# Two weight loads of the first mixer's compression issued on SyncE's queue instead of ScalarE's

## The chip, the cores and the metric

The kernel runs on one core of a Trainium2 chip. The metric is the device time of one execution in microseconds, the median of the runs of one program. TensorE (PE in the profile), VectorE (DVE), ScalarE (ACT), GpSimd (POOL) and SyncE (SP) each run their own instruction list and meet only at semaphores. Loads from device memory are issued by SP, ACT or POOL and moved by the core's 16 DMA engines.

## The reference, cut to what matters

The program is a stack of transformer-like blocks over 256 tokens of width 1024 in float32. The change lies in the first mixer, `nsa_attention`. It projects the normed input with one large weight matrix, and two of the results are compressed by a small network whose first weights are `w1_k` and `w1_v`, 2048 x 256 each, 2 MB apiece in float32:

```
proj = h @ w_in                      # 1024 x 2608, loaded in 11 pieces ("units")
q, kc, vc, ks, vs, kwn, vwn, gl = jnp.split(proj, splits, axis=-1)
def compress(t, pe, w1, w2):
    blk = t[:, tok_idx] + pe[:, None, :]
    blk = jnp.moveaxis(blk, 3, 2).reshape(B, n_c, N_KV, CMP_BLOCK * HEAD_DIM)
    return jax.nn.gelu(blk @ w1) @ w2
k_cmp = compress(kvh(kc), pe_k, w1_k, w2_k)
v_cmp = compress(kvh(vc), pe_v, w1_v, w2_v)
```

After this mixer come a feed-forward block, a second mixer with its feed-forward block, and a second model part of the same kind. None of that is touched.

## The kernel before

All large weights stream through one ring of three buffers of 1 MB (`RAW`, in the profile `raw_units`). A piece of weights is a unit, numbered over the whole program. Units 0 to 10 are those of `a_in`, the first mixer's projection: eight of 1 MB, then unit 8 of 192 KB (the gates), then two more of 1 MB. Each unit passes four stations in order:

- SP issues its load in `load_unit`; from unit 3 on it first waits for `lo_done`, the split of the unit three places earlier, because that frees the buffer.
- ACT copies it to a rounded high part in `split_hi` (line 170, `units_hi`), when it has landed and when TensorE has finished the unit three before.
- DVE subtracts to get the low part in `split_lo` (line 178, `units_lo`).
- TensorE multiplies: 48 matmuls per unit at lines 195 to 197, three per product.

ACT and DVE take their work strictly in the order written out in `project_a_scalar` and `project_a_vector`. There, the splits of units 3 and 4 come ahead of the copies of the first results out of PSUM (line 1083 on ACT, line 1136 on DVE), and TensorE waits for both copies before unit 4, since that unit's result overwrites the bank: `pe.wait_ge(m.s("a_left_out"), 1)` and `pe.wait_ge(m.s("a_right_out"), 1)` in `project_a_tensor`.

The compression's weights `W1K` and `W1V` are not part of the ring; they have their own place in SBUF. They are waited for once, in `compress_hidden_tensor` (line 216), which TensorE reaches after unit 7: `pe.wait_ge(m.s("w1_in"), 32)`. In the kernel before, ACT issues both loads in `compress_loads_scalar`, after it has copied the distance tables (lines 893 and 895) and ahead of the split of unit 3.

At the very start SP issues the two halves of x and units 0 to 2 with no wait. ACT at the same time issues nine small loads (the identity, the table inputs, seven rows of gains at line 829), and only then loads its function table and squares x for the norm (line 241). POOL issues some twenty small loads of constants.

Of the kernel before, what the change touches and what calls it, by code (L numbers as in the profile page):

```python
# [17 lines left out]
P = 128  # L18
# [67 lines left out]
def slot(n):  # L86
    return n % 3
# [57 lines left out]
def first_unit(stage):  # L145
    return [n for n, u in enumerate(UNITS) if u[0] == stage][0]
# [7 lines left out]
def load_unit(sp, m, n, parts):  # L154

    if n >= 3:
        sp.wait_ge(m.lo_done, n - 2)
    assert len(parts) == UNITS[n][1], (n, UNITS[n])
    for dst, src in parts:
        sp.dma_start(dst, src).then_inc(m.raw_landed[slot(n)], 16)  # L160
# [69 lines left out]
def norm_squares_scalar(act, m, k, src, junk, ready, tiles=range(TT)):  # L230

    sem, value, per_tile = ready
    n = TT * ROW_NORMS[k][0]
    for t in tiles:
        act.wait_ge(sem, value + per_tile * t)
        if junk is None:
            out = m.HN[:, t, :]
        else:
            out = junk
            act.wait_ge(m.s("norm_squared"), n + t)  # L240
        act.activation(out, src[:, t, :], ACT.Square,
                       accum_out=m.SS[:, t:t + 1]).then_inc(m.s("norm_squared"), 1)
# [42 lines left out]
def norm_turned_scalar(act, m, k, g, outs, second=0, gains=False):  # L285

    if gains:
        act.wait_ge(m.s("gains_set"), 1)
    for b in range(4):
        act.wait_ge(m.s("norm_transposed"), 4 * ROW_NORMS[k][0] + b + 1)  # L290
        if second:
            act.wait_ge(m.s("norm_lo"), ROW_NORMS[k][1] + b + 1)
        for kt in (2 * b, 2 * b + 1):
            hi, src = turned_rows(m, k, g, b, kt, outs[0][:, kt, :])
            ins = act.activation(hi, src, ACT.Copy, scale=m.GC[:, g * KT + kt:g * KT + kt + 1])
        ins.then_inc(m.s("norm_hi"), 1)
# [521 lines left out]
def first_loads_scalar(act, m):  # L818

    i = m.i  # L820
    act.dma_start(m.IDENT[:, :], i["c_ident"]).then_inc(m.s("ident_in"), 16)
    act.dma_start(m.HOT, i["c_hot"]).then_inc(m.s("table_inputs_in"), 16)
    gains = [(i["norm_mix"], 2), (i["norm_ffn"], 2), (i["kv_norm"], 1), (i["ffn1_norm_2"], 1), (i["mem_norm_2"], 1),
             (i["mix_norm_2"], 1), (i["ffn2_norm_2"], 1)]
    assert len(gains) == N_GAINS
    g = 0
    for src, n in gains:
        rows = src.rearrange("(k p) -> k p", p=P) if len(src.shape) == 1 else src.rearrange("g (k p) -> (g k) p", p=P)
        act.dma_start(m.GROW[g * KT:(g + n) * KT, :], rows).then_inc(m.s("gains_in"), 16)
        g += n  # L830
# [8 lines left out]
    pool.dma_start(m.RBI[:, :], i["rel_bias_2"]).then_inc(m.s("table_rows_in"), 16)  # L839


def compress_loads_scalar(act, m):

    i = m.i
    for dst, src in ((m.A.W1K, i["a_w1_k"]), (m.A.W1V, i["a_w1_v"])):
        act.dma_start(dst, src[0].rearrange("(u p) n -> p u n", p=P)).then_inc(m.s("w1_in"), 16)


def setup_vector(dve, m):
# [38 lines left out]
def tables_scalar(act, m):  # L888

    act.wait_ge(m.s("tables_made"), 2)  # L890
    w = W_ALL // 3
    for c in range(3):
        act.activation(m.TAB16[:, c * w:(c + 1) * w], m.pb[4 + c][0:HEADS, 0:w], ACT.Copy)\
            .then_inc(m.s("tables_copied"), 1)
    act.activation(m.TAB8, m.pb[7][0:8, 0:W_IDX], ACT.Copy).then_inc(m.s("tables_copied"), 1)
# [59 lines left out]
def project_a_sync(sp, m):  # L955
    w = m.i["a_w_in"][0].rearrange("(k p) n -> p k n", p=P)
    n = first_unit("a_in")
    for c in range(5):
        if c == 4:
            load_unit(sp, m, n, [(m.RAW[:, slot(n), 0:KT * 48].rearrange("p (k c) -> p k c", k=KT),  # L960
                                  w[:, :, 2560:2608])])
            n += 1
        for half in range(2):
            load_unit(sp, m, n, [(m.RAW[:, slot(n), :].rearrange("p (k c) -> p k c", k=4),
                                  w[:, 4 * half:4 * half + 4, c * 512:(c + 1) * 512])])
            n += 1


def project_keys_a_tensor(pe, m, n, bank):
# [531 lines left out]
def attend_a_scalar(act, m):  # L1501
    def out_hi(T):
        act.wait_ge(m.s("a_summed"), 2 * (LAST_PAIR[T] + 1))
        act.activation(m.OTH[:, T, :], m.pb[6 + T % 2][:, 0:S], ACT.Copy).then_inc(m.s("a_out_hi"), 1)

    for p in range(2, NPA + SUM_AFTER):
        for T in range(7):
            if LAST_PAIR[T] + 4 == p:
                out_hi(T)
        if p < NPA:  # L1510
            exp_pair_a_scalar(act, m, p)
        if TURN_AFTER <= p < NPA + TURN_AFTER:
            i = p - TURN_AFTER
            for par in range(2):
                act.wait_ge(m.s("a_turned"), 2 * i + par + 1)
                if i >= 2:
                    act.wait_ge(m.s("a_summed"), 2 * (i - 1))
                act.activation(m.A.PT[:, i % 2, par, :], m.pb[4 + par][:, 0:3 * P], ACT.Copy)\
                    .then_inc(m.s("a_turned_copied"), 1)
    out_hi(7)  # L1520
# [1915 lines left out]
def hybrid_transformer_kernel(nc, i, out):  # L3436
    with ExitStack() as ctx:
        m = Names()
# [25 lines left out]
        @block.sync  # L3464
        def _(sp):
            first_loads_sync(sp, m)
            project_a_sync(sp, m)
            out_sync(sp, m, "a_out", i["a_w_out"][0])
            ffn_sync(sp, m, 0, i["ffn_w_up"][0], i["ffn_w_down"][0])
            project_b_sync(sp, m)  # L3470
            out_sync(sp, m, "b_out", i["b_w_out"][0])
            ffn_sync(sp, m, 1, i["ffn_w_up"][1], i["ffn_w_down"][1])
            ffn_sync(sp, m, 2, i["ffn1_w_in_2"][0], i["ffn1_w_out_2"][0])
            memory_sync(sp, m)
            project_c_sync(sp, m)
            merge_sync(sp, m)
            mixer_out_sync(sp, m)
            ffn_sync(sp, m, 3, i["ffn2_w_in_2"][0], i["ffn2_w_out_2"][0])
            for t in range(TT):
                store_half(sp, m, out, t, 0)  # L3480
            sp.wait_ge(m.s("stored"), 16 * 2 * TT)
# [35 lines left out]
        @block.scalar  # L3517
        def _(act):
            first_loads_scalar(act, m)
            for t in range(TT):  # L3520
                norm_squares_scalar(act, m, 0, m.XR, None, (m.x_in[t], 16, 0), (t,))
            split_ahead(act, m, split_hi, "a_in", 0, 1)
            norm_turned_scalar(act, m, 0, 0, HT, gains=True)
            split_ahead(act, m, split_hi, "a_in", 1, 3)
            tables_scalar(act, m)
            compress_loads_scalar(act, m)
            project_a_scalar(act, m)
            attend_a_scalar(act, m)
            split_ahead(act, m, split_hi, "a_out", 1, 4)
            split_ahead(act, m, split_hi, "ffn0", 0, 2)  # L3530
            tile_scalar(act, m, 0)
            ffn_scalar(act, m, 0)
            split_ahead(act, m, split_hi, "b_in", 0, 2)
            norm_halves_scalar(act, m, 2, 2)
            norm_turned_scalar(act, m, 2, 4, HT)
            project_b_scalar(act, m)
            attend_b_scalar(act, m)
            split_ahead(act, m, split_hi, "b_out", 1, 4)
            split_ahead(act, m, split_hi, "ffn1", 0, 2)
            tile_scalar(act, m, 1)  # L3540
            ffn_scalar(act, m, 1)
            split_ahead(act, m, split_hi, "ffn2", 0, 2)
            state_step_scalar(act, m)
            tile_scalar(act, m, 2)
            ffn_scalar(act, m, 2)
            norm_turned_scalar(act, m, 5, 6, HT)
            split_ahead(act, m, split_hi, "mem_kv", 0, 2)
            norm_halves_scalar(act, m, 6, 6)
            split_ahead(act, m, split_hi, "c_in", 0, 1)
            norm_turned_scalar(act, m, 6, 7, OT)  # L3550
            memory_scalar(act, m)
            split_ahead(act, m, split_hi, "c_in", 1, 2)
            state_turn_scalar(act, m)
            inner_c_scalar(act, m)
            mix_c_scalar(act, m)
            split_ahead(act, m, split_hi, "c_out", 2, 4)
            split_ahead(act, m, split_hi, "ffn3", 0, 2)
            tile_scalar(act, m, 3)
            ffn_scalar(act, m, 3)
            final_norm_scalar(act, m)  # L3560
            for t in range(TT):
                store_half(act, m, out, t, 1)
# [75 lines left out]
def split_ahead(eng, m, split, stage, first, last):  # L3638

    for j in range(first, last):  # L3640
        split(eng, m, first_unit(stage) + j)
# [29 lines left out]
```

## Time and profile before

| | us |
|---|---|
| median of 3 runs | 1306.37 |
| lowest, highest run | 1306.25, 1306.43 |
| span of the profiled execution | 1303.1 |
| median less the span | 3.3 |
| TensorE busy in the span | 1270.1 |
| VectorE, ScalarE busy | 811.3, 644.9 |
| ScalarE's issue of the second load of compression weights | 4.92 |

Only the span is known of the profiled execution; its own device time is not listed, so the 3.3 us outside the span are taken from the median of the runs. Three runs lie within 0.2 us of each other. All times below count from the span's start. The first mixer takes the first 144 us.

### The profile page before, as it was taken

Reading aid. Unit: us, or ns where it says so; the run is one execution under the profiler, and the core shown is the slowest. Engines: PE = TensorE matmul, PEld = TensorE weight load, DVE = VectorE, ACT = ScalarE, POOL = GpSimd, SP = SyncE. Lnnn points to the kernel's source line nnn. Section 1 sums busy time; section 2 is a strip of 40 time slices with the busy share of each in tenths; the row PEclk is TensorE's granted clock in tenths of the full one; section 3 lists DMA queues with packets and bytes.
Section 4 is the critical chain, followed back from the end, with each engine's and each line's share of the span. In section 5 each row is a group of like instructions: output and inputs, shape, how many; then the busy total and the mean of one; then the engine's idle time right before and its main releaser. Section 6 shows DMA issues by size and latency. Waiting matters only on the chain.

```text
span 1303.1 us, 19302 instructions
## 1 busy us (share of the span) xinstructions
PE 1270.1 (97%) x7279; PEld 1059.4 (81%) x7279; DVE 811.3 (62%) x1210; ACT 644.9 (49%) x946; POOL 271.3 (21%) x362
## 2 busy tenths in 40 slices
PE   6999999999999999999999999999999999999997
PEld 5986788888799977888888788888887778888886
DVE  3468675555574486654555755556789877755554
ACT  4438654444453366543444655445444683544442
POOL 6420210000000041102000489701186210200000
PEclk9999999999999999999999999999999999999999
DMA  9970556555455644467655465654544436556651
GB/s 288 273 136 19 166 173 193 182 184 186 159 194 180 177 115 130 161 195 175 228 183 179 167 194 186 220 188 147 194 130 146 146 121 202 181 190 193 191 188 41
DMA packets 155883, 224.77 MB, mean 172 GB/s; under 512 B 13395, under 2 KB 107979, under 8 KB 155820
## 3 DMA queue, kind: packets, MB, share of 16 engines
q1 hardware_dynamic: 141008, 208.36, 50.9%
q0 software_dynamic: 10064, 10.54, 4.3%
q10 hardware_dynamic: 4748, 5.02, 1.1%
q8 instruction: 41, 0.67, 0.2%
q14 instruction: 22, 0.18, 0.0%
HBM read 222.56 MB, written 1.25 MB: 172 GB/s over the span
## 4 chain that ended last, share of the span: by engine, by line
PE 80%; DVE 8%; ACT 4%; DMA 4%; issue 2%; POOL 1%; SPq 0%; DVEq 0%; ACTq 0%; POOLq 0%
PE bank L195 23%; PE bank L197 23%; PE bank L196 23%; PE bank L216 4%; DMA raw_units<-in_a_w_in 3%; DVE units_lo L178 3%; PE bank L204 2%; PE bank L702 1%; DMA raw_units<-in_ffn_w_up 1%; ACT arena L1497 1%; DVE arena L2907 1%; PE bank L211 1%; PE bank L1774 1%; DVE arena L2898 1%; ACT units_hi L170 1%
## 5 line engine op out<-in xcount | busy, mean ns | idle before, releaser
L621 DVE TENSOR_TENSOR units_lo<-raw_units,units_hi 128x2048 fp32r<-128x2048 f32 x96 | 223.1, 2324 | 154.2 <-ACT units_hi L575 154.2
L195 PE MATMUL bank<-units_hi,turned_hi 128*128 128x512 f32 (+1 forms) x792 | 307.0, 388 | 3.1 <-DVE units_lo L178 1.3
L197 PE MATMUL bank<-units_hi,turned_lo 128*128 128x512 f32 (+1 forms) x792 | 302.1, 381 | 0.0
L196 PE MATMUL bank<-units_lo,turned_hi 128*128 128x512 f32 (+1 forms) x792 | 301.7, 381 | 0.0
L178 DVE TENSOR_TENSOR units_lo<-raw_units,units_hi 128x2048 fp32r<-128x2048 f32 (+2 forms) x103 | 232.4, 2265 | 109.3 <-ACT units_hi L170 109.1
L170 ACT ACTIVATE units_hi<-raw_units 128x2048 fp32r<-128x2048 f32 (+2 forms) x103 | 193.2, 1886 | 113.3 <-PE bank L197 83.1
L575 ACT ACTIVATE units_hi<-raw_units 128x2048 fp32r<-128x2048 f32 x96 | 183.5, 1911 | 104.0 <-PE bank L197 95.6
L195 PE MATMUL bank<-units_hi,second_hi 128*128 128x512 f32 (+1 forms) x560 | 219.2, 391 | 0.0
L197 PE MATMUL bank<-units_hi,second_lo 128*128 128x512 f32 (+1 forms) x560 | 216.8, 387 | 0.0
L196 PE MATMUL bank<-units_lo,second_hi 128*128 128x512 f32 (+1 forms) x560 | 216.6, 387 | 0.0
L195 PEld LDWEIGHTS bank<-units_hi,turned_hi 128*128 128x128 f32 x792 | 149.0, 188 | 32.8 <-DVE units_lo L178 3.0
L197 PEld LDWEIGHTS bank<-units_hi,turned_lo 128*128 128x128 f32 x792 | 148.9, 188 | 29.2
L196 PEld LDWEIGHTS bank<-units_lo,turned_hi 128*128 128x128 f32 x792 | 149.2, 188 | 26.9
L195 PEld LDWEIGHTS bank<-units_hi,second_hi 128*128 128x128 f32 x560 | 105.4, 188 | 23.4 <-issue 1.7
L197 PEld LDWEIGHTS bank<-units_hi,second_lo 128*128 128x128 f32 x560 | 105.3, 188 | 21.6
L196 PEld LDWEIGHTS bank<-units_lo,second_hi 128*128 128x128 f32 x560 | 105.6, 189 | 20.5
L585 ACT ACTIVATE second_hi<-bank 128x512 fp32r<-128x512 f32 x44 | 26.3, 599 | 127.6 <-PE bank L702 127.6
L261 POOL TENSOR_SCALAR means<-sums 128x1 f32<-128x1 f32 x6 | 2.1, 357 | 363.4 <-ACT rows L249 363.4
L627 DVE SCALAR_TENSOR_TENSOR rows<-rows,bank 128x256 f32<-128x256 f32 x88 | 36.9, 419 | 57.3 <-ACT rows L581 42.0
L635 DVE TENSOR_TENSOR second_lo<-bank,second_hi 128x512 fp32r<-128x512 f32 x44 | 30.4, 690 | 66.6 <-ACT second_hi L585 66.6
L195 PE MATMUL bank<-second_hi,units_hi 128*128 128x256 f32 x240 | 68.3, 285 | 0.0
L196 PE MATMUL bank<-second_lo,units_hi 128*128 128x256 f32 x240 | 67.9, 283 | 0.0
(352 smaller groups left out, 1789.8 us busy)
## 6 DMA issues: line engine op xcount, KB each, us to landing
raw_units<-in_ffn_w_up SPq DMA_DIRECT2D x88, 512.0 KB, 4.8
raw_units<-in_ffn_w_in SPq DMA_DIRECT2D x88, 512.0 KB, 4.6
raw_units<-in_ffn_w_down SPq DMA_DIRECT2D x22, 1024.0 KB, 4.9
raw_units<-in_ffn_w_out SPq DMA_DIRECT2D x22, 1024.0 KB, 4.9
raw_units<-in_w_in SPq DMA_DIRECT2D x18, 1024.0 KB, 5.0
raw_units<-in_b_w_q SPq DMA_DIRECT2D x12, 1024.0 KB, 5.2
raw_units<-in_a_w_in SPq DMA_DIRECT2D x10, 1024.0 KB, 10.7
raw_units<-in_kv_w SPq DMA_DIRECT2D x6, 1024.0 KB, 5.2
```

Of the source, the lines that this page charges most:

```text
L170: act.activation(hi, raw, ACT.Copy).then_inc(m.hi_done, 1)
L178: dve.tensor_tensor(lo, raw, hi.bitcast(F32), ALU.subtract).then_inc(m.lo_done, 1)
L195: pe.matmul(out, lh, rh, start=start, stop=False, skip_group_check=True)
L196: pe.matmul(out, lh, rl, start=False, stop=False, skip_group_check=True)
L197: return pe.matmul(out, ll, rh, start=False, stop=True, skip_group_check=True)
L204: ins = pe.matmul(out, *((rows_hi, w) if stationary else (w, rows_hi)), start=start and x == 0, stop=False, skip_group_check=True)
L216: return pe.matmul(out, lhsT, rhs, start=start, stop=stop, skip_group_check=True)
L575: act.activation(m.WH[:, slot(n0 + j), :], m.RAW[:, slot(n0 + j), :], ACT.Copy).then_inc(m.hi_done, 1)
L585: act.activation(turned(m.OTH, s), m.pb[TR_BANK][:, :], ACT.Copy).then_inc(hi, 1)
L621: dve.tensor_tensor(m.WL[:, slot(n0 + j), :], m.RAW[:, slot(n0 + j), :], m.WH[:, slot(n0 + j), :].bitcast(F32), ALU.subtract).then_inc(m.l ...
L627: dve.scalar_tensor_tensor(out=m.UU[:, t, :], in0=m.TH[:, t, :], scalar=1.0, in1=m.pb[t][:, 0:FSTEP], op0=ALU.add, op1=ALU.mult).then_inc( ...
L635: dve.tensor_tensor(turned(m.OTL, s), m.pb[TR_BANK][:, :], turned(m.OTH, s).bitcast(F32), ALU.subtract)\
```

## The change

The function that issued both loads on ACT's queue is gone. `compress_load_sync` issues one of them on SP's queue, `W1K` right behind unit 2 (the third unit) and `W1V` right behind unit 3 (the fourth). Both carry the same semaphore as before, and TensorE's wait for them is the same.

```
-def compress_loads_scalar(act, m):
-
-    i = m.i
-    for dst, src in ((m.A.W1K, i["a_w1_k"]), (m.A.W1V, i["a_w1_v"])):
-        act.dma_start(dst, src[0].rearrange("(u p) n -> p u n", p=P)).then_inc(m.s("w1_in"), 16)
+def compress_load_sync(sp, m, x):
+
+    dst, src = ((m.A.W1K, m.i["a_w1_k"]), (m.A.W1V, m.i["a_w1_v"]))[x]
+    sp.dma_start(dst, src[0].rearrange("(u p) n -> p u n", p=P)).then_inc(m.s("w1_in"), 16)
...
@@ project_a_sync
             n += 1
+            if n - first_unit("a_in") in (3, 4):
+                compress_load_sync(sp, m, n - first_unit("a_in") - 3)
...
@@ the list of ACT's work
             tables_scalar(act, m)
-            compress_loads_scalar(act, m)
             project_a_scalar(act, m)
```

On SyncE, at the start of the program, the rows before are (here `in_a_w_in` is the projection's weights, x8 eight units in a row, the first three of which wait for nothing):

```order
L795 DMA residual<-in_x 128x1024 x2
L160 DMA raw_units<-in_a_w_in 128x4x512 x3
L160 DMA raw_units<-in_a_w_in 128x4x512 [waits lo_done] x5
L160 DMA raw_units<-in_a_w_in 128x8x48 [waits lo_done]
L160 DMA raw_units<-in_a_w_in 128x4x512 [waits lo_done] x2
```

and the same place now, with `in_a_w_k` and `in_a_w_v` the compression's weights:

```order
L795 DMA residual<-in_x 128x1024 x2
L160 DMA raw_units<-in_a_w_in 128x4x512 x3
L845 DMA arena<-in_a_w_k 128x16x256
L160 DMA raw_units<-in_a_w_in 128x4x512 [waits lo_done]
L845 DMA arena<-in_a_w_v 128x16x256
L160 DMA raw_units<-in_a_w_in 128x4x512 [waits lo_done] x4
L160 DMA raw_units<-in_a_w_in 128x8x48 [waits lo_done]
L160 DMA raw_units<-in_a_w_in 128x4x512 [waits lo_done] x2
```

The first load stands ahead of SP's first wait, the second behind it; every unit from unit 3 on now stands behind 2 MB of other data, and from unit 4 on behind 4 MB.

On ScalarE, from the copies of the tables on, the rows before are:

```order
L893 ACTIVATE tables<-bank 16x509 x2
L895 ACTIVATE tables<-bank 8x383
L846 DMA arena<-in_a_w_k 128x16x256
L846 DMA arena<-in_a_w_v 128x16x256
L170 ACTIVATE units_hi<-raw_units 128x2048 x2
L1083 ACTIVATE arena<-bank 128x512
```

and now:

```order
L892 ACTIVATE tables<-bank 16x509 x3
L894 ACTIVATE tables<-bank 8x383
L170 ACTIVATE units_hi<-raw_units 128x2048 x2
L1084 ACTIVATE arena<-bank 128x512
```

Nothing stands between the last table copy and the splits of units 3 and 4 (the x2 at line 170).

## Rows read from the trace of the kernel before

**Rows 1.** Window, length, busy us: PE, PEld, DVE, ACT, POOL; clock, DMA share.
```profile
16.00:98.00 82.00, 81.56 (x662) 75.95 (x663) 43.45 (x74) 31.88 (x47) 32.44 (x51) 0.98 0.97 221
```
**Rows 2.** Waits of TensorE's matmuls from 16 to 98 us: total, times, longest.
```profile
PE bank L195 <- DVE turned_lo L327: 1.1, 1, 1.1
```
**Rows 3.** Chain that ended last, 14 to 80 us: start, us, what.
```profile
27.49 3.51 issue
...
37.53 15.02 DMA raw_units<-in_a_w_in
```
**Rows 4.** Timeline of ScalarE, 25.5 to 38 us: start, us, what, idle before.
```profile
26.04 4.92 ACTq L846 DMA_DIRECT2D arena<-in_a_w_v  x1
...
31.06 3.72 ACT L170 ACTIVATE units_hi<-raw_units 128x2048 fp32r<-128x2048 f32 x2 [3.57 <-issue]
```
**Rows 5.** Timeline of VectorE, 30 to 110 us.
```profile
33.01 4.50 DVE L178 TENSOR_TENSOR units_lo<-raw_units,units_hi 128x2048 fp32r<-128x2048 f32 x2 [10.73 <-ACT units_hi L170]
37.42 0.68 DVE L1136 TENSOR_SCALAR arena<-bank 128x512 f32<-128x512 f32 x1
...
73.84 0.42 DVE L1251 COPY arena<-bank 128x256 f32<-128x256 f32 x1
```
**Rows 6.** Timeline of TensorE, 42.6 to 43 us: unit 4 begins.
```profile
42.85 0.28 PE L195 MATMUL bank<-turned_hi,units_hi 128*128 128x256 f32 x1
```
**Rows 7.** Timeline of TensorE, 58 to 98 us.
```profile
65.98 7.15 PE L216 MATMUL bank<-arena,rows 128*64 128x256 f32 x64
...
75.94 0.92 PE L216 MATMUL bank<-arena 64*128 64x256 f32 x8
76.95 0.44 PE L1201 MATMUL bank<-ident,arena 128*128 128x128 f32 x2
...
92.17 0.92 PE L216 MATMUL bank<-arena 64*128 64x256 f32 x8
93.03 0.39 PE L195 MATMUL bank<-units_hi,turned_hi 128*128 128x256 f32 x1
```
**Rows 8.** DMA issues, 2.97 to 3.03 us (unit 2): KB, us to landing.
```profile
raw_units<-in_a_w_in SPq DMA_DIRECT2D x1, 1024.0 KB, 13.5
```
**Rows 9.** DMA issues, 25.5 to 26.5 us.
```profile
arena<-in_a_w_k ACTq DMA_DIRECT2D x1, 2048.0 KB, 11.5
```
**Rows 10.** DMA queues, 16.5 to 37.1 us: packets, MB (q1 SP's, q10 ACT's).
```profile
q1 hardware_dynamic: 1551, 3.08, 44.6%
q10 hardware_dynamic: 2765, 2.82, 40.2%
```
**Rows 11.** DMA queues, 15.2 to 17.2 us.
```profile
q1 hardware_dynamic: 148, 0.28, 73.2%
```
**Rows 12.** DMA queues, 20 to 22.3 us (q0 POOL's).
```profile
q0 software_dynamic: 102, 0.11, 99.2%
q1 hardware_dynamic: 11, 0.01, 2.6%
```
**Rows 13.** DMA queues, 31 to 37 us.
```profile
q10 hardware_dynamic: 1995, 2.03, 98.5%
```
**Rows 14.** DMA queues and issues, 602 to 608 us; no other queue is listed.
```profile
q0 software_dynamic: 50, 0.00, 67.4%
...
raw_units<-in_ffn_w_up SPq DMA_DIRECT2D x3, 512.0 KB, 12.7
```
**Rows 15.** Timeline of ScalarE, 2 to 12 us.
```profile
2.21 0.85 ACTq L829 DMA_DIRECT2D tables<-in_norm_ffn  x1
...
4.65 0.33 ACTq L829 DMA_DIRECT2D tables<-in_ffn_norm  x1
5.01 1.28 ACT L241 ACT_TABLE_LOAD   x1 [5.01 <-issue]
...
10.50 1.91 ACT L170 ACTIVATE units_hi<-raw_units 128x2048 fp32r<-128x2048 f32 x1 [1.70 <-DMA raw_units<-in_a_w_in]
```
**Rows 16.** Timeline of SyncE's issues, 0 to 4 us.
```profile
1.66 1.89 SPq L160 DMA_DIRECT2D raw_units<-in_a_w_in  x3
```

## The prediction, made before the changed kernel was run

> **What bounds the kernel now.** I looked first at the chain that ended last, because it seems to name the very thing the change removes: in the first mixer it holds 3.51 us of issue time on ScalarE, followed by a wait of 15.02 us for a projection unit [rows 3]. The timeline of ScalarE shows what that is. The issue of the second load of compression weights takes 4.92 us, from 26.04 to 30.96, and the split of units 3 and 4 behind it starts at 31.06 after 3.57 us of idleness [rows 4]. Read alone, this promises some 3.5 us.
>
> The view to set against it is TensorE's. From 16 to 98 us it is busy 81.56 of 82 us [rows 1], and its matmuls wait for another engine once in that stretch, for 1.1 us at its very start [rows 2]. A chain is followed back through whatever came last at each step, even where it came before it was needed; a stall on it is worth only what its consumer waits. So I price every step by the slack ahead of TensorE.
>
> **The stall that goes: 0 us.** Without the two issues ScalarE begins the split of unit 3 at 31.06 - 3.57 = 27.49, so 3.6 us earlier. Who needs it? VectorE subtracts units 3 and 4 in one stretch from 33.01 to 37.51, 2.25 us each [rows 5], so unit 3 is ready at about 35.3. TensorE begins unit 4 at 42.85 [rows 6]; a unit is 48 matmuls at a spacing of 0.12, or 5.76 us, so it begins unit 3 at 37.1. Unit 3 was 1.8 us early already. The copy out of PSUM that unit 4 also needs ends on VectorE at 37.42 + 0.68 = 38.10 [rows 5], 4.75 us early. The work that hides the stall is TensorE's own, units 1 and 2. Were that cover gone, the stall would cost up to 3.6 us.
>
> **The bytes that move ahead: 0 us, between 0 and +1.1.** Here the slack is spent. Before, units 3 to 5 had SP's queue to themselves and the compression weights came after them; the first of those landed at 25.59 + 11.5 = 37.1 [rows 9]. Now unit 4 is behind both. How long SP's and ACT's queues would take for it can be counted from the landing of unit 2 at 2.99 + 13.5 = 16.5 [rows 8]. Ahead of and including unit 4 stand 2.10 + 1.05 + 2.10 + 1.05 = 6.29 MB. From 16.5 to 37.1 the two queues moved 3.08 + 2.82 = 5.90 MB [rows 10]. The missing 0.39 MB go at 2.03 MB in 6 us, that is 0.34 MB/us [rows 13], which makes 1.2 us more: 38.3.
>
> Two holes may be filled. From 15.2 to 17.2 SP's queue moved 0.28 MB where 0.68 would fit [rows 11], since unit 3 was issued only at about 14.8; the compression weights now stand ready there, so 0.40 MB or 1.2 us come back: 37.1. From 20 to 22.3 it moved 0.01 MB [rows 12]; that would be another 2.3 us, down to 34.8. But POOL's constants held the engines for 99.2% of that hole. The nearest like case is 602 to 608 us: SP's units had been issued, POOL's small packets took 67.4% of the engines, and not one packet of SP's queue moved [rows 14]. I count the second hole as lost. Against that, the last DMA engine is behind the mean: the last byte of the first compression load landed at 37.1, when on average the engines had already moved 5.90 - 5.24 = 0.66 MB of the next one, 1.9 us of work. Unit 4 has therefore landed on the last engine between 34.8 and 37.1 + 1.9 = 39.0; I take 37.8.
>
> From landing to TensorE: 1.9 us on ScalarE (half of 3.72), 2.25 on VectorE, 0.68 for the copy behind it, 4.9 with the hops. So unit 4 must have landed by 37.95. At 37.8 nothing waits, at 39.0 TensorE waits 1.1 us. I take 0.1. Unit 3 is the end of the first 3.15 of the 6.29 MB, so it lands some 9 us ahead of unit 4, near 29, where 37.1 less 4.2 for its two splits, or 32.9, would do. Unit 5 lands 3.1 us behind unit 4 and is needed 5.76 us behind it, so it is safer than unit 4. From unit 6 on everything is earlier than before, as no compression weights are left to share with: they are both down by about 35, and TensorE wants them at 65.98 [rows 7].
>
> By its queue rule the Trainium skill agrees on the order: DMA: Bandwidth & Descriptors, Queues, rings and completion order, says each DMA engine takes the descriptors of one issuer's ring in order and goes round between issuers' rings. By that rule the old arrangement shared between ACT's and SP's loads, and the new one is first come, first served.
>
> **A small gain: -0.15 us, between -0.7 and 0.** TensorE starts the turn of the hidden layer at 76.95, 1.01 us behind the start of a score group, while the same group at 92.17 is followed after 0.86 [rows 7]: a wait of 0.15. It is for a gelu chain that VectorE starts at 73.84, right behind the split of unit 10 [rows 5]; the product it needs was over at 65.98 + 7.15 = 73.13. With units 6 to 10 earlier the chain can start 0.7 us earlier, and 0.15 of that is waited for.
>
> **SP's own queue: 0 us.** Two issues more. If each blocks SP for 4.92 us as on ACT [rows 4], the first does so from 3.55 [rows 16] to 8.5, and SP has nothing to issue before 14.8. The second holds up the issues of units 4 and 5, but behind 2 to 4 MB of queued work their turn comes later anyway.
>
> **Sum.** 1303.1 + 0.1 - 0.15 + 0 = 1303.05 in the span, plus 3.3 outside it, 1306.35. I say 1306.4: no change.
>
> **Rivals.**
>
> *Slower: ScalarE is held up at the start.* SP's first new issue stands at 3.55, and ScalarE is then still issuing its last four loads of gains, one of 0.33 at 4.65, ahead of its function table at 5.01 [rows 15]. If SP's blocked issue blocks ScalarE's too, until 8.5, those four end at about 9.8 instead of 4.98, 4.8 later. ScalarE has 1.70 us of idleness ahead of the split of unit 0 [rows 15], so that split, and with it TensorE's first projection, comes some 3.1 us later: 1309.5. It decides once the block lasts more than the 1.7 us of slack. For it: in the only moment when both queues were issuing under load, ScalarE's issue took 0.85 against 0.33 [rows 15], and SP's three took 1.89 together. Against it: ScalarE's later issues were short again while SP's units were still queued, and ACT's first load of compression weights was taken while SP's units were in flight. Chance 0.14.
>
> The Trainium skill speaks for this rival: Perfetto Trace Analysis, DMA Instruction — HWDGE (DVE, Sync), says the descriptor generator is shared and is locked for exclusive use until all of an issue's descriptors are made, which can be as long as the buffer is full. By that rule the sum is 1309.5; by the short issues in the trace it is 1306.4. No row has an SP issue stalled with ScalarE's waiting, so the trace leaves it open.
>
> *Slower: unit 4 is later still.* If POOL's constants, which now meet a full queue from 16.5 on, cost it 0.9 MB more, unit 4 lands at 40.6 and TensorE waits over 2.6 us: 1309. For it, 99.2% in rows 12; against, that was already counted once. Chance 0.04.
>
> *Faster: the chain is right.* If TensorE does wait where matmul ends are only modelled, the 3.5 us come back: 1302.9. Against it stands an even spacing of 0.12 us on to unit 4. Chance 0.03.
>
> **How the numbers follow.** The measurement tells about 0.2%, 2.6 us, from no change. The forecast has 0.79, with its own range of 1305.5 to 1307.6: the gain's bound of -0.7 with some scatter below, the wait's +1.1 above. Reaching partly into the first rival takes it to 1305.4 to 1309.2. Same 0.79 and 0.01 of the rivals' weak forms, faster 0.03, slower 0.17.
>
> **What the profile after would show.** Right: ScalarE's split of unit 3 near 27.5, unit 4's landing seen in its split at 36 to 39, compression weights landed by 35, TensorE beginning its projection at 16.4 and unit 4 at 42.85, its busy time from 16 to 98 unchanged, the gelu chain 0.7 us earlier. Wrong: ScalarE's table load later than 5.1; a wait of a matmul at line 195 near 43; the later units not earlier. The prediction fails if issues on two queues hinder each other, or if the DMA engines move much less from 16.5 to 38.

## The result, and the profile after

The changed kernel takes 1311.84 us, median of 4 runs (1309.58 to 1313.36); the kernel before takes 1306.40 us in 4 runs (1306.25 to 1308.04). The ratio is 1.0036, 95% interval 1.0022 to 1.0049: about 4.7 us slower (the two medians taken alone differ by 5.4). The profiled execution is the quickest of the four, 1309.58 us with a span of 1307.8, against 1303.1 before. The forecast was 1306.4 with a range to 1309.2, so it was wrong, on the slower side, which it had given a chance of 0.17.

TensorE is where the time must show. The window over the same stretch as [rows 1], with the same columns:

```profile
16.00:98.00 82.00, 79.62 (x619) 74.10 (x620) 39.75 (x53) 28.57 (x36) 34.57 (x51) 0.98 0.88 217
```

It is busy 1.94 us less (81.56 before). Its waits from 16 to 98 us, which answer to [rows 2]:

```profile
PE bank L216 <- POOL rows L1175: 2.2, 1, 2.2
```

There was no such wait at line 216 before. Line 216 is `compress_hidden_tensor`, and the 64 matmuls there wait for rows that POOL builds (`blocks_ready`). The timeline of TensorE shows the places where it falls behind:

```profile
26.62 0.39 PE L195 MATMUL bank<-turned_hi,units_hi 128*128 128x256 f32 x1
...
44.07 0.36 PE L195 MATMUL bank<-turned_hi,units_hi 128*128 128x256 f32 x1
...
69.51 8.83 PE L216 MATMUL bank<-arena,rows 128*64 128x256 f32 x64 [2.18 <-POOL rows L1175]
78.27 0.32 PE L195 MATMUL bank<-turned_hi,units_hi 128*48 128x256 f32 x1
```

The first row begins unit 1, and the second unit 4, which began at 42.85 before [rows 6], so it is 1.22 late. The third begins the hidden layer, 65.98 before [rows 7], so 3.53 late. The 64 matmuls take 8.83 us instead of 7.15, another 1.7 us. Together that makes 5.2 us at this point; the span ends 4.7 later, and where the other 0.5 comes back was not traced. The windows on both sides of 73.2 us say why they are slow (the clock is the third number from the end):

```profile
69.80:73.20 3.40, 3.40 (x20) 2.39 (x18) 2.29 (x1) 0.00 (x0) 3.40 (x5) 0.50 0.25 42
73.20:76.60 3.40, 3.40 (x34) 2.73 (x32) 0.00 (x0) 0.00 (x0) 0.32 (x1) 0.99 0.65 144
```

Right after the idle time the granted clock is 0.50, that is 1.2 GHz instead of 2.4, and 20 matmuls run in 3.4 us where 34 run at full clock.

What is behind POOL's rows is read from the chain that ended last, which this time does name what was waited for:

```profile
20.36 18.75 DMA raw_units<-in_a_w_in
...
39.13 1.92 ACT units_hi L170
...
41.08 2.30 DVE units_lo L178
...
43.40 10.97 DMA raw_units<-in_a_w_in
...
54.39 1.92 ACT units_hi L170
...
56.33 2.29 DVE units_lo L178
...
61.54 0.22 POOL rows L1172
...
69.51 8.85 PE bank L216 x64
```

Unit 4 is issued at 20.36, lands at 39.11 behind the 4 MB of compression weights, and is split until 43.38. Only then is the buffer of unit 4 free for unit 7, whose load SP issues at 43.40; before it was issued at 37.53 [rows 3]. It lands at 54.4 (52.5 before). VectorE splits it from 56.33, and behind that split, in program order, stand its four copies of the values out of PSUM (line 1123, 58.60 to 61.38), although the products that they copy, those of unit 5, were finished at 55.7. POOL waits for that copy, and begins at 61.54. In the kernel before, its timeline had it at 59.73, with two groups of four additions, and the rows were done at 65.6:

```profile
59.73 0.21 POOL L1171 MEMSET rows<- 128x64 f32 x1 [13.52 <-DVE arena L1122]
59.84 2.93 POOL L1174 TENSOR_TENSOR rows<-arena 128x240 f32<-128x240 f32 x4
...
62.82 2.78 POOL L1174 TENSOR_TENSOR rows<-arena 128x240 f32<-128x240 f32 x4
```

In the changed kernel POOL is then hit again, on its own timeline:

```profile
64.66 2.70 POOL L1175 TENSOR_TENSOR rows<-arena 128x240 f32<-128x240 f32 x1
...
67.32 0.71 POOL L1175 TENSOR_TENSOR rows<-arena 128x240 f32<-128x240 f32 x1
```

One addition takes 2.70 us, the next 0.71. The long one lies beside this row of VectorE, the split of unit 9:

```profile
64.25 2.54 DVE L178 TENSOR_TENSOR units_lo<-raw_units,units_hi 128x2048 fp32r<-128x2048 f32 x1 [2.27 <-ACT units_hi L170]
```

The addition begins 0.4 us behind the split's start and ends 0.6 us behind its end. In the kernel before this split came just behind the start of POOL's last addition, and it was the split that took longer:

```profile
64.91 2.83 DVE L178 TENSOR_TENSOR units_lo<-raw_units,units_hi 128x2048 fp32r<-128x2048 f32 x1 [4.75 <-ACT units_hi L170]
```

So the working theory, called the ring theory below, has these links: both loads ahead of unit 4; unit 4 split late; unit 7 issued late by the ring of three buffers; its transfer in the middle of POOL's ten bias loads (line 918, issued from 39.27 to 47.3); VectorE's copy and POOL's rows late; POOL's addition held up by VectorE; TensorE waiting and then at half clock. The bias loads were in flight beside unit 7 in the kernel before as well (issued from 38.22 us, and unit 7 took 15.0 us to land), but it had been issued 5.9 us earlier. The rivals are a start theory (only the first 26 us matter, since unit 1 begins 1.14 late), and a port theory (the meeting of POOL and VectorE is all there is).

### The profile page after: what moved, and what is told of

Same layout as the page of the kernel before. It is cut to its first block, busy times and chain, and to the rows that moved or that the text cites. A ratio compares the mean times of both kernels' runs of the same rounds, so it can differ in the third digit from the quotient of the medians.

```text
span 1307.8 us, 19302 instructions
## 1 busy us (share of the span) xinstructions
PE 1274.0 (97%) x7279; PEld 1062.3 (81%) x7279; DVE 811.6 (62%) x1210; ACT 644.7 (49%) x946; POOL 273.2 (21%) x362
## 4 chain that ended last, share of the span: by engine, by line
PE 82%; DVE 7%; ACT 4%; DMA 3%; POOL 2%; issue 1%; DVEq 0%; SPq 0%; POOLq 0%; ACTq 0%
PE bank L195 24%; PE bank L197 23%; PE bank L196 23%; PE bank L216 4%; DMA raw_units<-in_a_w_in 3%; DVE units_lo L178 3%; PE bank L204 2%; PE bank L702 1%; ACT arena L1498 1%; DVE arena L2908 1%; PE bank L211 1%; PE bank L1775 1%; DVE arena L2899 1%; POOL rows L1175 1%; DVE arena L2361 1%
## 5 line engine op out<-in xcount | busy, mean ns | idle before, releaser
L627 DVE SCALAR_TENSOR_TENSOR rows<-rows,bank 128x256 f32<-128x256 f32 x88 | 36.8, 419 | 57.5 <-ACT rows L581 42.1
L635 DVE TENSOR_TENSOR second_lo<-bank,second_hi 128x512 fp32r<-128x512 f32 x44 | 30.4, 690 | 66.6 <-ACT second_hi L585 66.6
```

Source lines behind the costliest of these rows:

```text
L627: dve.scalar_tensor_tensor(out=m.UU[:, t, :], in0=m.TH[:, t, :], scalar=1.0, in1=m.pb[t][:, 0:FSTEP], op0=ALU.add, op1=ALU.mult).then_inc( ...
L635: dve.tensor_tensor(turned(m.OTL, s), m.pb[TR_BANK][:, :], turned(m.OTH, s).bitcast(F32), ALU.subtract)\
```

## The experiments

In each run the kernel before was timed on the same chip. Its medians were 1307.54, 1306.80 and 1306.68 us in the three groups, and its runs spread from 1305.0 to 1311.2, more than the three runs shown at first suggested. Comparisons therefore go by ratios.

| kernel | us | ratio, 95% interval |
|---|---|---|
| after_again | 1311.07 | 1.0031 (1.0017 to 1.0044) |
| k_early | 1305.70 | 0.9990 (0.9982 to 0.9999) |
| v_early | 1311.81 | 1.0032 (1.0022 to 1.0042) |
| bias_late | 1307.63 | 1.0000 (0.9991 to 1.0008) |
| pool_k_first | 1307.10 | 1.0002 (0.9993 to 1.0010) |
| port_free | 1308.22 | 1.0012 (1.0003 to 1.0021) |
| before_unit7_late | 1313.78 | 1.0049 (1.0034 to 1.0065) |
| behind_unit5 | 1306.05 | 0.9995 (0.9986 to 1.0004) |
| v_one_later | 1306.01 | 0.9991 (0.9982 to 1.0000) |
| v_one_later_kfirst | 1306.07 | 0.9997 (0.9988 to 1.0006) |
| before_pool_k_first | 1305.96 | 0.9998 (0.9989 to 1.0007) |
| behind_unit5_kfirst | 1306.82 | 0.9999 (0.9987 to 1.0010) |

**after_again**: the changed kernel unaltered.

> The changed kernel again, unaltered, to have the spread of its runs beside the kernel before. Ring theory (both compression loads pass ahead of unit 4, so unit 4 is split 7.8 us later, so SP issues unit 7 at 43.4 instead of 37.5, in the middle of POOL's bias loads; unit 7, VectorE's copy of the values out of PSUM and POOL's rows for the compression are each late, and TensorE waits some 2.2 us at line 216 and then runs at half clock): 1309 to 1313, with the wait at line 216 in the profile each time. Start theory (the only lasting loss is the first 26 us: x lands 0.26 us later and unit 0 is multiplied more slowly): the wait at line 216 is incidental, and a second profile may well be without it.

The loss is there again, 1309.5 to 1314.24 in 7 runs. TensorE's waits in its profile:

```profile
PE bank L216 <- POOL rows L1175: 3.1, 1, 3.1
PE bank L195 <- DVE turned_lo L327: 1.5, 1, 1.5
PE bank L195 <- issue: 0.3, 1, 0.3
PE bank L1202 <- DVE arena L1262: 0.3, 1, 0.3
```

The wait at line 216 is no accident of one execution. Unit 1 began at 25.71 here, near the 25.48 of before, and the loss was no smaller: the first mark against the start theory. After this longer wait the clock stayed at 1.00 from 70 to 74 us, and the half clock came later:

```profile
86.00:92.00 6.00, 6.00 (x40) 5.68 (x40) 2.76 (x4) 0.00 (x0) 0.00 (x0) 0.72 0.92 213
```

**k_early and v_early**: one of the two loads on SP, the other back on ScalarE. The comments give the value in v_early.

```
-            if n - first_unit("a_in") in (3, 4):
-                compress_load_sync(sp, m, n - first_unit("a_in") - 3)
+            if n - first_unit("a_in") == 3:          # v_early: == 4
+                compress_load_sync(sp, m, 0)         # v_early: 1
...
             tables_scalar(act, m)
+            compress_load_sync(act, m, 1)            # v_early: 0
```

> Only W1K on SP behind unit 2; W1V on ScalarE at its old place. The start of the program is that of the changed kernel, but unit 4 stands behind 2 MB on SP and shares with W1V only from 26 us on. Start theory: x and the first projection are late as in the changed kernel, +1.1 us at unit 1 and lasting, 1307.5. Ring theory: unit 4 lands near 35 instead of 39.1, unit 7 is issued near 40, and whatever of POOL's bias loads (from about 39) it meets decides; the rows for the compression are in time or up to 1 us late: 1307 to 1309, less than the changed kernel's loss.

> Only W1V on SP behind unit 3; W1K on ScalarE at its old place. Nothing new is queued before 14.8 us. Start theory: x lands at 7.63 as before, unit 1 begins at 25.5 and the time is that of the kernel before, 1306.4. Ring theory: unit 4 stands behind 2 MB on SP and shares with W1K from 26 us on, lands near 34 to 36, and the time is between 1306.4 and 1308.5, by how much unit 7's issue slides into POOL's bias loads.

The two differ by far more than expected: W1K ahead costs nothing, W1V ahead of unit 4 costs everything. Both estimates missed: 1306.4 to 1308.5 was too low for v_early, and 1307 to 1309 was too high for k_early, which came out at the time of the kernel before. The issue of unit 7 with its KB and its time to landing, in k_early (window 36.6 to 36.8 us):

```profile
raw_units<-in_a_w_in SPq DMA_DIRECT2D x1, 1024.0 KB, 13.7
```

and in v_early (window 42.9 to 43.0 us):

```profile
raw_units<-in_a_w_in SPq DMA_DIRECT2D x1, 1024.0 KB, 13.6
```

The transfers are equally long; the issue is 6 us apart, because unit 4 landed by 32.4 in one and at 38.7 in the other. k_early has no wait at line 216; v_early has the second longest of all the profiles, in this row of TensorE:

```profile
71.72 9.35 PE L216 MATMUL bank<-arena,rows 128*64 128x256 f32 x64 [4.76 <-POOL rows L1175]
```

v_early queues nothing new in the first 14 us, and loses as much as the changed kernel: against the start theory again.

**before_unit7_late**: the kernel before, with one wait on SP.

```
@@ project_a_sync, in the loop over the units
+            if n - first_unit("a_in") == 7:
+                sp.wait_ge(m.unit_used, 4)
```

> The kernel before, but SP holds back the load of unit 7 until TensorE has finished unit 3, which is near 42.9 us instead of 37.5; nothing else is moved, and both compression loads stay on ScalarE. Ring theory: this alone brings the loss back without its start part: unit 7 lands near 54, the rows for the compression are late, TensorE waits about 2 us at line 216 (it arrives at 66) and runs some 3 us at half clock: +3 to +4.5 us, 1309.5 to 1311. Start theory: no change, 1306.4.

Unit 7 issued at 43.72 brings back the whole loss and more, +0.49%. Nothing of the start, of unit 4 or of the compression loads was touched. Unit 7 is not quite alone, though: SP issues in order, so the small load of unit 8 behind it also went later, at 44.13 instead of 41.62. Its row of TensorE:

```profile
74.09 9.60 PE L216 MATMUL bank<-arena,rows 128*64 128x256 f32 x64 [6.84 <-POOL rows L1176]
```

It is more than the 1309.5 to 1311 expected, for two reasons in its profile. Unit 7 took 13.2 us to land (56.9 us) and not 11.0 (54.4), for which the cause stays open, so POOL began at 64.09. And both halves of POOL's work met a split of VectorE: its timeline of POOL shows each group of four additions at 4.96 and 4.73 us, where 2.93 and 2.78 stand in the kernel before. The stretch at half clock that goes with the wait lasted 6.8 us here, twice as long as in the changed kernel.

**bias_late**: the changed kernel with POOL's ten bias loads held back.

```
             tables_gpsimd(pool, m)
+            pool.wait_ge(m.hi_done, first_unit("a_in") + 8)
             bias_a_gpsimd(pool, m, range(0, 10))
```

> The changed kernel, but POOL waits with its ten bias loads (line 918) until ScalarE has split unit 7, so that they no longer meet unit 7's load. Ring theory: unit 7, still issued at 43.4, lands near 48 instead of 54.4, VectorE's copy of the values follows unit 5's products at about 56, POOL builds the rows from 58 to 65, TensorE does not wait at line 216 (67.05) and its clock stays full there: 3.5 to 4 us less than the changed kernel, with only the start's +1.1 us left over the kernel before, 1307 to 1308. Port theory (the loss is POOL's addition held up by VectorE's split of unit 9, whatever made POOL late): the same gain if the two no longer meet, none if they still do. Start theory: no gain, 1309.5 to 1312.

Unit 7 is issued at 42.96, close to the 43.40 of the changed kernel (42.91 in after_again), and the time from issue to landing falls from 11.0 to 5.2 us. The DMA queues from 45 to 47 us, in the changed kernel:

```profile
q0 software_dynamic: 273, 0.33, 62.2%
q1 hardware_dynamic: 25, 0.05, 35.5%
```

and the same in bias_late:

```profile
q1 hardware_dynamic: 378, 0.77, 102.7%
```

Unit 7's issue in bias_late (window 43 to 43.5 us), us to landing last:

```profile
raw_units<-in_a_w_in SPq DMA_DIRECT2D x1, 1024.0 KB, 5.2
```

Beside POOL's packets SP's queue moved 0.05 MB, without them 0.77 MB. The loss shrinks from 4 us to nothing measurable. A wait of 0.8 us is left in the profile, where none was expected (the profiled run, 1309.37, is the second slowest of its twelve): POOL is now busy issuing until 60.2, and its addition again meets VectorE's split. So the collision with the bias loads is a necessary link.

**pool_k_first** lets POOL begin with the keys, which ScalarE copies early.

```
-    pool.wait_ge(m.s("a_left_out"), 3)
-    pool.wait_ge(m.s("a_right_out"), 3)
     for n, (dst, src) in enumerate(((m.A.RK, m.A.KC2), (m.A.RV, m.A.VC2))):
+        pool.wait_ge(m.s(("a_left_out", "a_right_out")[n]), 3)
```

> The changed kernel, but POOL builds the rows of the keys as soon as ScalarE has copied the keys, instead of waiting for VectorE's copy of the values too. In the changed kernel ScalarE's copy ends at 58.6 and VectorE's at 61.4. Ring theory: half of POOL's work goes ahead of 61.4, the rows are ready near 65 to 66 instead of 69.4, TensorE does not wait at 67.05: 3 to 4 us less, about 1308. If the first additions lose the shared port to VectorE's copies (58.60 to 61.38), 1 us of that is lost. Start theory: no change, 1309.5 to 1312.

POOL's start on the keys and its additions for the values, in its timeline:

```profile
58.68 0.21 POOL L1171 MEMSET rows<- 128x64 f32 x1 [12.05 <-ACT arena L1121]
...
61.61 3.04 POOL L1174 TENSOR_TENSOR rows<-arena 128x240 f32<-128x240 f32 x4
```

Unit 7 is as late as ever (its split begins on ScalarE at 54.35), yet the rows are ready at 64.6, nothing waits at line 216 and 1.0002 is left. So the loss passes through POOL's rows, as far as 0.1% can be told.

**port_free** keeps VectorE's split of unit 9 away from POOL's additions.

```
     split_lo(dve, m, n + 8)
+    dve.wait_ge(m.s("blocks_ready"), 2)
     split_lo(dve, m, n + 9)
```

> The changed kernel, but VectorE waits for POOL's rows before it splits unit 9, so that no VectorE split runs beside POOL's additions. Port theory: the addition that took 2.70 us beside the split takes 0.73 again, the rows are ready at about 67.4 instead of 69.4, TensorE's wait falls from 2.4 to about 0.3 us and its clock stays full: 2 to 3.7 us less, about 1306.5 to 1308; unit 9's split ends some 3.5 us later, near 70, and is not needed before 80. Ring theory alone: the wait shrinks by no more than 0.5, 1309 to 1312.

TensorE at the hidden layer, in its timeline:

```profile
67.70 7.15 PE L216 MATMUL bank<-arena,rows 128*64 128x256 f32 x64 [0.72 <-POOL rows L1176]
```

The wait falls from 2.18 to 0.72 us (0.3 was expected) and the 64 matmuls run at full clock. The ratio goes from 1.0031 to 1.0012, so about 2.5 us of the loss came with the held-up addition; the two intervals just overlap, so that figure is rough. But 1.0012, with an interval that excludes 1, is left, and it too has its stretch of half clock, later (its windows 86 to 88 and 88 to 90 us show 0.56 and 0.59). The port theory has a large part and is not the whole.

**behind_unit5**: both loads on SP, behind unit 5.

```
+            if n - first_unit("a_in") == 6:
+                compress_load_sync(sp, m, 0)
+                compress_load_sync(sp, m, 1)
```

> Both compression loads on SP, right behind unit 5 instead of behind units 2 and 3. Ring theory: units 3 to 5 land as early as or earlier than in the kernel before, W1K and W1V behind them by about 43, unit 6 behind those; unit 7 is issued when unit 4 is split, near 37; if it lands by 55 nothing waits: 1306.4, the kernel before. If unit 6 or 7 behind 4 MB is late, +1 to +4. Start theory: 1306.4, since nothing new is queued at the start.

0.9995. Its unit 1 begins at 26.02, although nothing new was queued ahead of it:

```profile
26.02 0.39 PE L195 MATMUL bank<-turned_hi,units_hi 128*128 128x256 f32 x1
```

Over all profiles this start lies between 25.5 and 26.8, in kernels of either kind, and the 25.48 of before is the earliest. Two variants that leave the start of the kernel before as it was have 26.15 (before_unit7_late) and 26.77 (before_pool_k_first). So the 1.14 us that I first read as the change's lie within the scatter of single executions.

**v_one_later**: the changed kernel with one number altered, W1V behind unit 4.

```
-            if n - first_unit("a_in") in (3, 4):
-                compress_load_sync(sp, m, n - first_unit("a_in") - 3)
+            if n - first_unit("a_in") in (3, 5):
+                compress_load_sync(sp, m, (n - first_unit("a_in") - 3) // 2)
```

> The changed kernel with one number altered: W1V on SP behind unit 4 instead of behind unit 3; W1K stays behind unit 2. Everything about the start is that of the changed kernel, and both loads are still on SP's queue, 4 MB ahead of unit 5. Ring theory: unit 4 lands near 32.5 as when W1K alone was moved, its split frees the buffer near 36.7, unit 7 is issued there, ahead of POOL's bias loads, and lands by 51; the rows are ready in time, TensorE does not wait at line 216: 1305.5 to 1307, the loss is gone. Theory that the bytes ahead of the later units matter in sum: unit 5 now lands near 40 and unit 7 is behind all 4 MB as before, so most of the loss stays, 1309.5 to 1311.

0.9991. The issue of unit 7 in its timeline of SP:

```profile
36.93 0.37 SPq L160 DMA_DIRECT2D raw_units<-in_a_w_in  x1
```

Its timeline of POOL, the two groups of four additions:

```profile
58.70 3.09 POOL L1175 TENSOR_TENSOR rows<-arena 128x240 f32<-128x240 f32 x4
...
61.84 4.84 POOL L1175 TENSOR_TENSOR rows<-arena 128x240 f32<-128x240 f32 x4
```

Its timeline of TensorE at the hidden layer, with no idle time ahead of the row:

```profile
67.05 7.16 PE L216 MATMUL bank<-arena,rows 128*64 128x256 f32 x64
```

Unit 7 is issued at 36.93. POOL's addition is held up just as in the changed kernel (4.84 us for four), and costs nothing, because POOL began at 58.6 and is done at 66.6, 0.4 us ahead of TensorE. The same 4 MB stand ahead of unit 5 and the units behind it as in the changed kernel, and both loads are still on SP's queue; one place in it decides.

**The three with the keys first** (v_one_later_kfirst, before_pool_k_first, behind_unit5_kfirst: the edit of pool_k_first on those kernels) asked for a better version and for the spread of the kernel before.

> As the kernel with W1V behind unit 4, and POOL builds the rows of the keys as soon as ScalarE has copied them. Ring theory: no wait was left at line 216, so the keys first can give at most what runs lose that come near the deadline: within 0.1% of the same kernel without it. If the spread of the runs of the kernel before (1305.1 to 1310.4) comes from its rows being ready only 0.4 us ahead of TensorE in the profile, this one should have a narrower spread and a median of 1305 to 1306.

> The kernel before, but POOL builds the rows of the keys as soon as ScalarE has copied them. In the profile of before the rows were ready at 65.6 and TensorE came at 66.0. Edge theory (some runs of the kernel before miss that by a little and pay for a wait and half clock): median 1305.5 and fewer runs above 1308. Otherwise: the same median and the same spread as the kernel before.

> Both compression loads on SP behind unit 5, and POOL builds the rows of the keys as soon as ScalarE has copied them. This arrangement had no wait at line 216 and its rows were ready at 65.0 against 66.5. Edge theory: 1305 to 1306 with a narrow spread. Otherwise: 1306, as without the keys first.

None of the three can be told from the kernel before. Two had a narrower spread than before (1304.8 to 1306.9 and 1305.7 to 1307.4, against 1305.0 to 1311.2), the third had not (1305.2 to 1310.3). They have 11 runs each against its 33, and v_one_later without the keys first was as narrow (1304.8 to 1307.4), so this says nothing for the keys first. Whether some runs of the kernel before miss POOL's rows, which in its profile were ready 0.4 us ahead, stays open. No version beats the kernel before by more than 0.1%: k_early has 0.9990, with an interval that ends at 0.9999.

## Why the prediction was wrong

**The failed step** is the sentence "From unit 6 on everything is earlier than before, as no compression weights are left to share with". It counts bytes and forgets the ring. A unit from 3 on is issued only when the unit three places ahead is split; I had priced unit 4's landing against the one consumer that I saw, TensorE at 42.85, and found 4.9 us of work and 0.15 us of slack. Its second consumer is SP's wait for `lo_done`, which releases unit 7. That one has no slack: unit 7 was issued at 43.40 instead of 37.53. By my own numbers (landing 37.8, then 1.9 and 2.25) it would have come out at 42.0, and the question what is in the DMA engines then would have shown POOL's bias loads. v_one_later and before_unit7_late show this link in both directions. What the late issue cost was 1.9 us at unit 7's landing, and from there, in the profile, 2.2 us of waiting at line 216 and 1.7 at half clock.

Neither of the two failures that the prediction named came: issues on two queues did not visibly hinder each other (below), and SP's queue moved 5.86 MB from 16.5 to 37.1 us, where the two queues had moved 5.90.

**The bytes that move ahead, 0 us between 0 and +1.1.** The size of this term as priced was nearly right. Unit 4 landed at 39.11, where I took 37.8 and bounded it at 39.0; unit 4 on TensorE was held by less than 0.1 us in the profiled run. A landing by 39.1 and not by 37.95 was enough there, because TensorE itself was 1.14 us later: that was luck of this execution. after_again, where TensorE was only 0.2 us later, has a wait of 0.3 in this place.

**The stall that goes, 0 us: right.** ScalarE split unit 3 at 29.38, when it had landed, and nobody gained by it. The sign that I gave for it, a split near 27.5, did not fit my own landing of unit 3 near 29.

**The small gain, -0.15: nothing.** In v_one_later, where VectorE is free when the product ends, the gelu chain does begin at once, but TensorE's turn of the hidden layer still follows 1.01 us behind the start of the score group. VectorE's row in v_one_later says why:

```profile
75.17 1.10 DVE L1256 TENSOR_SCALAR arena<-arena 128x256 f32<-128x256 f32 x1
```

together with POOL's beside it:

```profile
75.17 0.96 POOL L1183 MEMSET arena<- 128x1024 f32 x1
```

POOL's two fills begin when the product ends, as the chain does. In the kernel before, the chain ran 0.7 us behind the product, and this operation met only the last 0.3 us of the second fill:

```profile
74.75 0.45 DVE L1255 TENSOR_SCALAR arena<-arena 128x256 f32<-128x256 f32 x1
```

```profile
74.10 0.96 POOL L1182 MEMSET arena<- 128x1024 f32 x1
```

In both kernels it ends some 0.15 us behind the end of that fill, and 2.1 us behind the product: what the chain gained by its earlier start was lost at POOL's fill.

**SP's own queue, 0 us:** no wait of TensorE leads to it, and the rival that leaned on it was wrong. SP in the timeline of the changed kernel:

```profile
3.50 3.18 SPq L845 DMA_DIRECT2D arena<-in_a_w_k  x1
```

and ScalarE at the same time:

```profile
3.98 0.31 ACTq L829 DMA_DIRECT2D tables<-in_mem_norm  x1
4.32 0.32 ACTq L829 DMA_DIRECT2D tables<-in_mix_norm  x1
4.67 0.34 ACTq L829 DMA_DIRECT2D tables<-in_ffn_norm  x1
5.04 1.28 ACT L241 ACT_TABLE_LOAD   x1 [5.04 <-issue]
```

SP's issue lasts from 3.50 to 6.68, and three of ScalarE's begin and end inside it at 0.31 to 0.34 us each; the table load is at 5.04, 5.01 before [rows 15]. The issue of unit 4 even took 8.67 us, but ScalarE issued no load beside it, so it tests nothing between the two. The slower outcome came, 2.3 us beyond the 1309.5 that this rival gave, by a mechanism that none of the rivals named. The rule of the Trainium skill (Perfetto Trace Analysis, DMA Instruction — HWDGE (DVE, Sync)) that an issue locks the shared generator did not show here as a block of ScalarE. That is all these rows say: they do not show when within its 3.18 us SP's issue held the generator.

**The sum's 3.3 us outside the span.** In every execution with both figures the time is 1.75 to 1.88 us more than the span, so the profiled execution of the kernel before took about 1304.9 (an estimate, 1303.1 + 1.8), and was quicker than the three runs listed. The 3.3 brought its span up to the median all the same, so this did not move the forecast. The 0.2 us between those three runs also gave too small an idea of the spread. The second rival's landing at 40.6 should by its own rates have been 40.5, a wait of 2.5 us; nothing hangs on it.

**What I had ready and did not use.** The timeline of before showed POOL's rows ready at 65.6 for TensorE's 65.98, and POOL's bias loads from 38.2. Both lie in the stretch that I called safe.

How the 5.2 us at 78.27 come about in the one profile: 1.14 at the start, put down to scatter, 0.1 at unit 4, 2.2 waiting for POOL's rows and 1.7 at half clock. Of the rows' delay of 3.8 us (69.4 against 65.6), 1.8 are unit 7's late landing and 2.0 the held-up addition. Shown by experiment are the ring's link, the bias loads, the passage through POOL's rows and a part of about 2.5 us of the held-up addition with what follows it. Not separated are wait and half clock: between 23 and 110 us, the six profiles with a wait at line 216 all have a stretch at half clock (3.4 us, or 6.8 behind the two longest waits), and the eight without that wait have none. That they go together is shown, not how the one brings on the other. Left open is also why the half clock follows at once in three of these executions and 18 to 19 us later in the other three.

## What to carry to other kernels

When a transfer is moved ahead of a unit in a ring of buffers, price it against both users of the unit: the engine that computes with it, and the load that waits for its buffer. Then ask what else is in the DMA engines at the moment when that later load will be issued. An engine that waits almost nowhere can stand 0.4 us away from a wait, as TensorE did here at line 216, and the list of waits does not show it; look up for each of its semaphores when it was set.

## What the hardware showed that I had not expected

- One load of 1 MB took 5.2 us from issue to landing with POOL's bias loads held back, and 11.0 us when issued at nearly the same moment beside them. In 2 us of that, POOL's queue moved 273 packets (0.33 MB) and SP's 25 (0.05 MB). From 47 to 54.4 us, POOL's queue was served beside it with 1233 packets to SP's 1277.
- A POOL addition of 0.71 to 0.74 us took 2.70 us beside VectorE's split, and ended 0.6 us behind it. In the kernel before the same meeting went the other way: POOL's addition kept its 0.73, and the split took 2.83 us instead of 2.29. The Trainium skill (SBUF — State Buffer, SBUF: two separate sides) says that a VectorE operation with two inputs in SBUF and a GpSimd operation that reads SBUF exclude each other for a whole instruction, and that whichever begins first wins; the trace agrees with that rule (the addition began 0.41 us behind the split in the changed kernel, and 0.03 ahead of it in the one before).
- VectorE's tensor_scalar took 0.45, 0.72, 0.90 and 1.10 us in four executions, the longer the earlier it began within POOL's second fill, and in all profiles it ended 0.14 to 0.16 us behind the fill's end. The Trainium skill (SBUF — State Buffer, Who interferes with whom) counts tensor_scalar among the operations that can exclude GpSimd; these rows agree with it.
- An issue on SP lasted 3.18 and 8.67 us with several MB of SP's earlier loads ahead of it, where 0.37 us is the usual. Three issues of ScalarE inside the 3.18 us kept to 0.31 to 0.34; beside the 8.67 us there was none.
- TensorE's granted clock fell to 0.50 for 3.4 us right behind a wait of 2.2 us in one execution. Behind a wait of 3.1 us in another it stayed at 1.00 and fell only near 88.6 us, again for 3.4 us.
